# Splitting the weights of two moved products behind the gate group, and two selection rounds moved ahead of and into the head norms, in a hybrid attention block on one core

## The reference

```python
h = rmsnorm(x, norm_w)
aq, ak, av, ag, bq, bk, bv, bg, iq, ik, iw = split(h @ w_in)
# group A: 4 heads of differential attention
p  = softmax(q1 k1 * scale + bias) - lam * softmax(q2 k2 * scale + bias)
ao = rmsnorm(p @ v, subln_w) * (1 - lambda_init)      # the head norm
ao = ao * silu(ag)
# group B: 8 heads; a query sees only 256 keys
score = sum_h iw_h * relu(iq_h . ik)                  # chunk-causal
sel   = top_k(score, 256)
bo    = softmax(q k[sel] * scale + bias) @ v[sel] * silu(bg)
out   = rmsnorm(x + concat(ao, bo) @ w_out)
```

## Time and profile before

| | |
|---|---|
| Median of 3 runs | 797.35 us (795.86 to 798.42) |
| Profiled execution | 797.5 us, span of its trace 795.3 us |
| TensorE (PE) busy | 758.3 us, 95% |
| VectorE (DVE) busy | 613.6 us, 77% |
| GpSimd (POOL) busy | 319.2 us, 40% |
| ScalarE (ACT) busy | 304.8 us, 38% |
| Chain that ended last | PE 64%, DVE 22%, POOL 5%, issue 3%, ACT 3%, DMA 2% |

### The profile page before, as it was taken

The page is one execution under the profiler, slowest core; times in us unless marked ns, Lnnn a source line. Parts: engine busy times, 40 slices in busy tenths (PEclk is TensorE's granted clock), DMA queues, the critical chain, the costliest instruction groups (busy, mean ns, idle before and its releaser), DMA issues.

```text
span 795.3 us, 11730 instructions
## 1 busy us (share of the span) xinstructions
PE 758.3 (95%) x4161; PEld 634.8 (80%) x4161; DVE 613.6 (77%) x1300; ACT 304.8 (38%) x677; POOL 319.2 (40%) x383
## 2 busy tenths in 40 slices
PE   4999999999999989999999999998999999899996
PEld 3765888888888878889888888886888888888885
DVE  3738999999998959878699999995767667534343
ACT  5437222031315546667520312106545455422221
POOL 5320122224534958761355553557996500300000
PEclk9999999999999989999999999999999999999998
DMA  7242111111102020021112111200311100121231
GB/s 277 55 120 66 40 45 48 54 43 51 53 15 53 0 54 19 10 79 44 43 50 54 40 53 54 67 14 26 107 41 67 28 2 1 47 100 67 92 106 53
DMA packets 24560, 44.54 MB, mean 56 GB/s; under 512 B 3076, under 2 KB 9912, under 8 KB 24376
## 3 DMA queue, kind: packets, MB, share of 16 engines
q1 hardware_dynamic: 24504, 43.81, 18.6%
HBM read 35.40 MB, written 6.57 MB: 53 GB/s over the span
## 4 chain that ended last, share of the span: by engine, by line
PE 64%; DVE 22%; POOL 5%; issue 3%; ACT 3%; DMA 2%; SPq 0%; DVEq 0%; ACTq 0%; POOLq 0%
PE psum L1100 20%; PE psum L1266 11%; PE psum L1205 10%; DVE score L1431 9%; DVE top L1426 9%; PE psum L1187 5%; PE psum L1162 4%; PE psum L1165 4%; PE psum L1000 3%; PE psum L1028 3%; PE psum L1044 1%; DMA k_high_twice<-k_high_twice 1%; ACT probsT_B L867 1%; DMA xs<-in_x 1%; PE psum L949 1%
## 5 line engine op out<-in xcount | busy, mean ns | idle before, releaser
L558 POOL TENSOR_TENSOR w_lo<-w_raw,w_hi 128x512 fp32r<-128x512 f32 x60 | 77.9, 1300 | 226.8 <-ACT w_hi L713 226.4
L1431 DVE MATCH_REPLACE8 score<-top,score 128x768 f32<-128x768 f32 (+5 forms) x176 | 157.3, 906 | 0.0
L1426 DVE MAX8 top<-score 128x8 f32<-128x768 f32 (+5 forms) x176 | 148.2, 909 | 1.1
L713 ACT ACTIVATE w_hi<-w_raw 128x512 fp32r<-128x512 f32 x60 | 37.7, 630 | 221.2 <-PE psum L1100 208.8
L856 ACT ACTIVATE probs<-psum,small 128x384 f32<-128x384 f32 (+7 forms) x128 | 94.9, 742 | 52.7 <-DVE small L1450 36.0
L1100 PE MATMUL psum<-w_hi,big_hi 128*128 128x512 f32 x256 | 99.6, 389 | 0.0
L1100 PE MATMUL psum<-w_lo,big_hi 128*128 128x512 f32 x256 | 99.6, 389 | 0.0
L1100 PE MATMUL psum<-w_hi,big_lo 128*128 128x512 f32 x256 | 99.6, 389 | 0.0
L1205 PE MATMUL psum<-v,probsT_B 128*128 128x64 f32 x576 | 74.8, 274 | 3.7 <-ACT probsT_B L867 2.6
L1205 PEld LDWEIGHTS psum<-v,probsT_B 128*128 128x128 f32 x576 | 70.4, 192 | 7.9 <-ACT probsT_B L867 3.6
L1100 PE MATMUL psum<-big_hi,w_hi 128*128 128x512 f32 x192 | 74.8, 390 | 0.0
(11 more groups left out here) (172 smaller groups left out, 1574.6 us busy)
## 6 DMA issues: line engine op xcount, KB each, us to landing
w_raw<-in_w_in SPq DMA_DIRECT2D x62, 256.0 KB, 2.6
xs<-in_x SPq DMA_DIRECT2D x8, 512.0 KB, 6.4
k_high_twice<-k_high_twice SPq DMA_DIRECT2D x16, 256.0 KB, 3.8
xres<-in_x SPq DMA_DIRECT2D x8, 512.0 KB, 3.5
out_y<-y_out SPq DMA_DIRECT2D x16, 256.0 KB, 2.1
w_tail<-in_w_out SPq DMA_DIRECT2D x10, 256.0 KB, 2.6
bias_scratch<-bias_row SPq DMA_DIRECT2D x1, 2304.0 KB
bias<-bias_scratch SPq DMA_DIRECT2D x12, 128.0 KB, 3.2
```

Source lines behind the costliest of these rows:

```text
L558: pool.tensor_tensor(lo[:, 0:cols], w_staged(n)[:, 0:cols], hi[:, 0:cols].bitcast(f32), ALU.subtract).then_inc(w_lo_made, 1)
L713: act.activation(w_parts(n)[0][:, 0:cols], w_staged(n)[:, 0:cols], ACT.Copy).then_inc(w_hi_made, 1)
L1426: ins = dve.max(top8[:, i - SEL0, :], sc)
L1431: ins = dve.match_replace(sc, top8[:, i - SEL0, :], sc, TAKEN)
```

## The change

Raw data of chunks Q0 and Q0 + 1 now lies in one row of the `probs` buffer (slot 1), and that of Q0 + 2 and Q0 + 3 in `w_raw[:, 0]`. SP loads Q0 and Q0 + 1 ahead of the gate group's last two chunks, with no wait. ScalarE does `high(Q0 + 1)` right behind `high(Q0)`, after the gate group's last chunk, and no longer in step 0 of phase 0. Because slot 1 of `probs` is written by the exponential of step 1, that waits for the split of Q0 + 1. The load of Q0 + 3 goes behind the key copy of block 2 and waits for the split of Q0 + 2. On VectorE one selection round is put between the last `finishA` and the wait for the squares, and one between `varA` and the wait for the root; the loop behind has two rounds less.

```diff
-    wf_raw, _ = place("wf_raw", [P, WIDTH], f32)
+    wf_raw, _ = place("wf_raw", [P, 2, WIDTH], f32, at=probs_at + ROW)
@@ w_staged
             if n in FILLS:
-                return w_raw[:, 0, :] if n % 2 == 0 else wf_raw[:, :]
+                return wf_raw[:, n - Q0, :] if n < Q0 + 2 else w_raw[:, 0, :]
@@ load_chunk, SP
-                if n == Q0:
+                if n in (Q0 + 2, Q0 + 3):
                     wait_split(sp, n - 1)
-                elif n in FILLS and n >= Q0 + 2:
-                    wait_split(sp, n - 2)
                 elif n == Q0 + 5:
-                    wait_split(sp, Q0 + 2)
+                    wait_split(sp, Q0 + 3)
@@ SP
-            for n in range(DB + SW, Q0 + 2):
+            for n in range(DB + SW, Q0 - 2):
                 load_chunk(n)
+            load_chunk(Q0)
+            load_chunk(Q0 + 1)
+            load_chunk(Q0 - 2)
+            load_chunk(Q0 - 1)
             copy_keys(0, 0)
             copy_keys(0, 1)
             load_chunk(Q0 + 2)
+            copy_keys(0, 2)
             load_chunk(Q0 + 3)
-            copy_keys(0, 2)
             copy_keys(0, 3)
@@ project, ScalarE
                         if g == A_GROUPS[-1] and d == DB - 1:
                             high(Q0)
+                            high(Q0 + 1)
@@ exp, ScalarE
                 act.wait_ge(max_ready, u + 1)
 
+                if ph == 0 and m == 0 and s == 1:
+                    wait_split(act, Q0 + 1)
@@ loop of phase 0, ScalarE
-                if s == 0:
-                    high(Q0 + 1)
-                elif s == 13:
+                if s == 13:
                     high(Q0 + 2)
@@ VectorE, behind phase 0
             finishA(STEPS - 2)
             finishA(STEPS - 1)
+            select(1, SEL0 + 1)
             dve.wait_ge(o_squared, STEPS)
             link(dve.tensor_scalar(ssA, ssA, 1.0 / P, EPS, ALU.mult, ALU.add))
             dve.tensor_copy(t_a[:, 0:1], ssA[:, 0:1]).then_inc(varA, 1)
+            select(1, SEL0 + 1)
             dve.wait_ge(rootA, 1)
             inverse_root(rA, ssA, rstdA, iw[:, 0:STEPS])
             dve.wait_ge(bias_loaded, 16 * nh)
             link(dve.memset(bias[0:CHUNK, A_HEADS:nh, BAND - CHUNK:BAND], MASKED))
-            select(ROUNDS - FIRST - 1, SEL0 + 1)
+            select(ROUNDS - FIRST - 3, SEL0 + 1)
```

## The result

The changed kernel takes 789.36 us in the median (788.67 to 790.18, four runs), the kernel before 797.88 beside it: ratio 0.9899, interval 0.9881 to 0.9917, so 8.1 us faster by the ratio (6.6 to 9.5 by its interval; the plain difference of the two medians is 8.5). I had forecast 788.6 from 797.35, 8.8 us. The sum was nearly right, but its two terms were not: one part gave more than I had reckoned, the other a third of it.

What follows compares the result with a forecast made beforehand. VectorE was taken to bound the stretch behind phase 0, TensorE nearly level, with late keys stalling TensorE between blocks 0 and 1. Gains of 6.3 + 2.5 = 8.8 us take 797.35 to 788.6 us, range 786.0 to 792.3.

Steps and rivals of the forecast that it cites:

- The stall: Border of blocks 0 and 1 in phase 0: TensorE's idle time for the keys goes, gaining 3.54 us.
- The clock: TensorE behind that idle time: the granted clock no longer falls to 0.51 for 5.63 us, gaining 2.76 us.
- The contention: Phase 0, GpSimd's moved splits beside VectorE work: net taken as 0, bounded by 1.30 us in either direction.
- part 1: Early split of chunk Q0 + 1 in phase 0: 3.54 us of idle time plus 2.76 of clock, 6.3 us.
- The second way to part 1: Phase 0: if block 0 (39.92 us) becomes like block 1 (32.56 us), 7.4 us go; kept for the range.
- The rounds: VectorE at the end of phase 0: moved selection rounds cover 2.60 us of idle time; gain taken as 2.5 us.
- The costs of the rounds: Projections behind phase 0: varA 9.2 us later, high(Q0 + 7) ending at 401.0, TensorE's chunk keeping 3.0 us of cover.
- The stall at the second chunk of group 6: TensorE in the projections: GpSimd's low half ends at 416.8, wanted at 416.1; new idle of up to 0.7 us.
- the rounds give nothing: Rival: TensorE's projections become the bound, stalling 2.3 us or more at group 6; gain 6.3 us, 791.0 us; chance 0.10.
- block 0 becomes wholly like block 1: Rival: phase 0 gains 7.4 us and the rounds all of 2.60; 787.4 us, or 786.1 with less contention; chance 0.13.

Runs made afterwards that it cites:

- busy stall: Kernel before, plus 16 unread matmuls on TensorE ahead of its wait for the keys of block 1: 795.59 us, ratio 0.9977.
- rounds-only: Kernel before with only the two selection rounds moved, loads and splits as before: 795.98 us, ratio 0.9982.
- ScalarE's copy: Changed kernel plus one 128x512 copy on ScalarE in step 0 of phase 0, where high(Q0 + 1) had stood: one run, 789.23 us.
- With the mask clear: Changed kernel with GpSimd splitting the query halves of phase 1's first block earlier, between weight chunks: 787.71 us, ratio 0.9881.

## Why the prediction was right, and where it was not

**The stall** (3.54 us) went as reckoned. The key halves end at 275.0 where I had 274.2. The steps on the way were off: GpSimd's query half waits for the gate group's last chunk on TensorE (2.03 us, to 251.89), a wait that stands in `split_part` and that I did not reckon. The wait for `o_tmp` behind it then shrank to 0.96 us where I had 1.7, so the end hardly moved.

**The clock** was the right mechanism, shown by the busy stall; its size is 1.6 to 2.3 us, not 2.76.

**The contention**, which I took at 0 with a bound of 1.30 in either direction, is the rest of part 1: 7.16 - 3.54 - 2.28 = 1.3 us of gain, the whole of my bound. Against the rounds-only trace it comes out the same: block 0 is shorter by 39.21 - 32.13 = 7.08 us there; less 3.52 for the pause and 1.57 for the clock that leaves 1.99, and 0.7 of it is given back ahead of the first combination. The first combination is 0.7 us later (255.99 against 255.31), as the rows of a split beside it said, and steps 1 to 4 then take 17.14 us (to 273.13) instead of 19.66 (to 274.97). VectorE's rows say where: from the first combination of block 0 to that of block 1 the combinations take 9.50 us instead of 9.92, and the small products ahead of them 3.06 instead of 5.71. ScalarE's copy does nothing, and in block 1 a shift of GpSimd's splits alone shortens the same instructions. So GpSimd's place is the cause by these two and by the rows; no run moved the splits of block 0 alone. The second way to part 1 in my text, 7.4 us from comparing blocks, came nearer than the sum that I preferred.

**The rounds** are the step that failed: I let VectorE's 2.60 us reach the mask and then priced the mask at its old 2.71 us, without looking at what would lie beside it when it moved. The gain up to the mask was 3.40 us, since the scaling and the inversion got quicker too; 2.60 of it was lost in the mask. With the mask clear the same rounds gave 2.74 us. The Trainium skill had it, in the section that I had cited ("SBUF — State Buffer", "Who interferes with whom"): copies and `tensor_scalar` can enter a mode that takes both ports and then contend with GpSimd. The Trainium skill frees an instruction with one input only outside these modes, a condition that my citation left out. I had used only the half on two inputs, and so held one-input instructions to be free. The trace agrees with the other half: one input, 5.31 us beside GpSimd and 2.71 alone. The selection rounds, one input too, stayed at 9.2 us beside GpSimd.

**The costs of the rounds** were right in kind and small. ScalarE's `high(Q0 + 7)` came at 391.02, GpSimd's half at 391.72, in time. The stall at the second chunk of group 6 that I put at up to 0.7 us is 0.3: chunks are freed at 409.01 and 414.74, 5.73 us apart instead of 5.44. It cost nothing, since TensorE had slack: it still waited 1.19 us for `mixB` behind the projections.

So the rival "the rounds give nothing" came nearly true, by another mechanism than the one I had named, and the rival "block 0 becomes wholly like block 1" came nearly true beside it. The two errors have opposite signs, and the total hides them: that 8.1 lies so near to 8.8 is luck.

## What to carry to other kernels

When a change makes an engine arrive earlier, price what it does next again at its new place: look which engine that shares something with it is at work there. Take idle time that is filled as a gain only up to the next such place. A pause of TensorE can cost more than its length, as the one of 3.54 us did; a busy wait shows how much, since it leaves the pause and removes the clock's part. Read such a size from more than one trace. And where two engines contend, shifting one engine's list by a step can be worth more than a removed wait.

## What the runs showed of the hardware

ScalarE loaded the table of the square root ahead of the wait that its activation had to keep, so the root came at once when `varA` did:

```profile
382.94 1.28 ACT L906 ACT_TABLE_LOAD   x1
390.89 0.23 ACT L906 ACTIVATE small<-small 128x32 f32<-128x32 f32 x1 [6.67 <-DVE small L1543]
```

I had charged 2.07 us for this way. The load lay beside the round instead, and `high(Q0 + 7)`, begun at 391.02, ended 10.6 us behind the last `o_tmp` where I had 12.8.

A pause of TensorE of 3.54 us was followed by 5.63 us at 0.51 of the clock. In the rounds-only kernel a pause of 3.52 us was followed by 3.66 us at 0.53. Pauses of 0.95 and 2.27 us in the kernel before were not followed by any lower clock.

A mask of six `tensor_scalar` instructions with one input took 2.71 us without GpSimd beside it and 5.31 to 5.39 beside its splits; the selection rounds, also with one input, took 9.2 us in both places. A product of 128x1 with two inputs took 0.22 us alone and up to 1.34 in block 0 of the kernel before.
